# Chunkwise mLSTM stage: steps written out, M rows spread by DMA, head-by-head exponentials and key weights on ScalarE

## Time and profile before

| | us |
|---|---|
| median of 3 runs | 1765.7 |
| the profiled execution, its device time | 1764.76 |
| its span in the trace | 1763.1 |
| the mLSTM block in it, from the last operation of `mlstm_gates` (415.7) to the first of `mlstm_norm` (545.3) | 129.6 |

### The profile page before, as it was taken

How to read it: one execution, slowest core, us unless ns; L and a number is a source line. 1 busy time by engine, 2 the same in 40 slices (tenths; PEclk the granted TensorE clock), 3 DMA queues, 4 the chain that set the end, 5 groups by cost and what they waited for, 6 DMA issues and landing times. The chain is left out here.

```text
span 1763.1 us, 20516 instructions
## 1 busy us (share of the span) xinstructions
PE 1534.4 (87%) x7374; PEld 843.3 (48%) x7375; DVE 605.9 (34%) x1060; ACT 331.0 (19%) x566; POOL 111.9 (6%) x113
## 2 busy tenths in 40 slices
PE   5999999957885798999899931999999999999968
PEld 1455544425773485665555521444444444444423
DVE  1222135435888333333376761011111111111107
ACT  1111122212223233343321110111111111111111
POOL 0000000000002000000000004011111111111100
PEclk7899999987987799999999955999999999999989
DMA  9101011050005102000041108687888987999937
GB/s 367 69 24 36 0 13 36 24 191 1 0 0 196 51 0 96 0 0 0 15 150 60 71 26 355 260 356 277 346 319 331 403 336 315 417 415 366 422 142 295
DMA packets 81139, 298.89 MB, mean 170 GB/s; under 512 B 18092, under 2 KB 28360, under 8 KB 71891
## 3 DMA queue, kind: packets, MB, share of 16 engines
q1 hardware_dynamic: 72356, 280.70, 40.7%
q0 software_dynamic: 8608, 16.84, 2.7%
q10 hardware_dynamic: 146, 0.98, 0.2%
HBM read 283.50 MB, written 25.73 MB: 175 GB/s over the span
## 5 line engine op out<-in xcount | busy, mean ns | idle before, releaser
L399 PE MATMUL ps<-w_in_tok,uT_tiles 128*128 128x512 f32 (+2 forms) x512 | 191.5, 535 | 1.2 <-ACT uT_tiles L320 1.2
L1712 PE MATMUL ps<-w_gate_sb,x_slotsT 128*128 x320 | 144.3, 604 | 9.7 <-issue 9.7
L1728 PE MATMUL ps<-w_down_sb,hidT 128*128 x320 | 148.0, 605 | 0.0
L399 PEld LDWEIGHTS ps<-w_in_tok,uT_tiles 128*128 128x128 f32 x512 | 97.7, 192 | 89.8 <-issue 61.1
L1712 PE MATMUL ps<-w_up_sb,x_slotsT 128*128 x320 | 140.6, 592 | 0.0
L1904 DVE TENSOR_TENSOR hid<-silu_g,ps 128x512 f32<-128x512 f32 x20 | 13.8, 688 | 294.4 <-PE ps L1712 294.4
L1419 PE MATMUL ps<-w_out,hT 128*128 128x512 f32 x256 | 114.2, 600 | 0.0
L480 PE MATMUL ps<-uT,mod 128*128 128x512 f32 x256 | 110.1, 592 | 1.7 <-ACTq L487 1.7
L1712 PEld LDWEIGHTS ps<-w_gate_sb,x_slotsT 128*128 128x128 f32 x320 | 59.8, 192 | 86.9 <-issue 86.9
L1712 PEld LDWEIGHTS ps<-w_up_sb,x_slotsT 128*128 128x128 f32 x320 | 60.8, 190 | 76.5 <-issue 76.5
L1728 PEld LDWEIGHTS ps<-w_down_sb,hidT 128*128 128x128 f32 x320 | 57.5, 189 | 66.5 <-issue 65.6
(11 more groups left out here) (377 smaller groups left out, 1966.9 us busy)
## 6 DMA issues: line engine op xcount, KB each, us to landing
light_gate_sb<-in_w_gate SPq DMA_DIRECT2D x20, 2048.0 KB, 11.4
light_up_sb<-in_w_up SPq DMA_DIRECT2D x20, 2048.0 KB, 16.5
light_down_sb<-in_w_down SPq DMA_DIRECT2D x20, 2048.0 KB, 13.1
w_gate_sb<-in_w_gate SPq DMA_DIRECT2D x12, 2048.0 KB, 11.5
w_up_sb<-in_w_up SPq DMA_DIRECT2D x12, 2048.0 KB, 15.9
w_down_sb<-in_w_down SPq DMA_DIRECT2D x12, 2048.0 KB, 21.5
uT<-in_w_ada SPq DMA_DIRECT2D x8, 2048.0 KB, 9.8
y_pair<-expert_rows SPq DMA_DIRECT2D x8, 1024.0 KB, 10.5
```

The lines of the kernel that those rows point to most:

```text
L399: mm = nc.tensor.matmul(ps[:, 2 + g, 0:n], uTt[:, j, k, :], wt[:, k, c0:c0 + n], start=k == 0, stop=k == KD - 1)
L1712: m = m_.matmul(ps[:, bank, :], xT[:, k, :], wt[:, bass.ds(buf, 1), k, :].rearrange("p a f -> p (a f)"), start=k == 0, stop=k == KD - 1)
L1728: m = m_.matmul(ps[:, 5 + half, :], hT[:, k, :], wd[:, bass.ds(buf, 1), k, half * 512:half * 512 + 512].rearrange("p a f -> p (a f)"), sta ...
```

The new lists, cut to their core (`HALVES` are the 16 pairs (i, d) in order, d innermost):

```diff
+                sp.wait_ge(s_rdy, 2)
+                sp.dma_start(self.md.rearrange("d h t -> h d t"), Mrow[:]).then_inc(s_mst, 16)
+                sp.wait_ge(s_mst, 16)
...
+            def _(sp):
+                for i, d in HALVES:
+                    if i > 0:
+                        sp.wait_ge(S["mm"][d], i)
+                        sp.wait_ge(S["a"][d], i)
+                    sp.dma_start(mb[:, d], self.md[d][:, cols(i, d)].partition_broadcast(P)).then_inc(s_mb[d], 16)
...
+                def decays(i, d):
+                    c = chunk(i, d)
+                    act.wait_ge(S["mm"][d], i + 1)
+                    if i > 0:
+                        act.wait_ge(S["p"][d], i)
+                    for h in range(H):
+                        op = a.activation(w[:, d, h, :], mm_[:, d, h, :], ACT.Exp, bias=self.acol[:, d, c, h:h + 1], scale=-1.0)
+                    op.then_inc(S["w"][d], 1)
+                    act.wait_ge(s_mb[d], 16 * (i + 1))
+                    if i > 0:
+                        act.wait_ge(S["q"][d], i)
+                    for h in range(H):
+                        op = a.activation(ab[:, d, h, :], mb[:, d, h, :], ACT.Exp, bias=self.mext[:, d, c + 1, h:h + 1], scale=-1.0)
+                    op.then_inc(S["a"][d], 1)
+
+                def keys(i, d):
+                    if i == TT - 1:
+                        return
+                    act.wait_ge(S["kt"][d], i + 1)
+                    if i > 0:
+                        act.wait_ge(S["cm"][d], i)
+                    for h in range(H):
+                        op = a.mul(kw[:, d, h, :], ps[:, 2, h * P:(h + 1) * P], self.wg[:, d, chunk(i, d), h:h + 1])
+                    op.then_inc(S["kw"][d], 1)
+
+                decays(0, 0)
+                decays(0, 1)
+                keys(0, 0)
+                keys(0, 1)
+                decays(1, 0)
+                for k in range(len(HALVES)):
+                    if k + 2 < len(HALVES):
+                        keys(*HALVES[k + 2])
+                    if k + 3 < len(HALVES):
+                        decays(*HALVES[k + 3])
...
+                def inner(i, d):
+                    if i > 0:
+                        pe.wait_ge(S["p"][d], i)
...  (scores to bank d)
+                    if d == 1:
+                        pe.wait_ge(S["kw"][0], i + 1)
+                    elif i > 0:
+                        pe.wait_ge(S["kw"][1], i)
...  (turned keys to bank 2)
+                def outer(i, d):
+                    pe.wait_ge(S["p"][d], i + 1)
+                    pe.wait_ge(S["q"][d], i + 1)
...  (and for cn of this direction, h of the half before; then the output as L798 to L801)
+                    pe.wait_ge(S["kw"][d], i + 1)
...  (and for cn of the half before; then the state product as L805 to L807)
+                inner(0, 0)
+                inner(0, 1)
+                pe.wait_ge(s_c0, 1)
+                for k, (i, d) in enumerate(HALVES):
+                    outer(i, d)
+                    if k + 2 < len(HALVES):
+                        inner(*HALVES[k + 2])
...
+                def masked(i, d):
+                    dve.wait_ge(s_mb[d], 16 * (i + 1))
+                    if i > 0:
+                        dve.wait_ge(S["w"][d], i)
+                    v.tensor_tensor(mm_[:, d], mb[:, d], self.c((C_MFW, C_MBW)[d]).unsqueeze(1).to_broadcast([P, H, P]), ALU.add).then_inc(S["mm"][d], 1)
...  (weighted: p and qs as L836 and L841; rows: as L849 to L852)
+                    for h in range(H):
+                        op = v.scalar_tensor_tensor(out=cst8[:, d, h, :], in0=cst8[:, d, h, :], scalar=self.dec[:, d, chunk(i, d), h:h + 1],
+                                                    in1=ps[:, 5 + h // 2, (h % 2) * hn:(h % 2 + 1) * hn], op0=ALU.mult, op1=ALU.add)
+                    op.then_inc(S["cn"][d], 1)
...
+                masked(0, 0)
+                masked(0, 1)
+                weighted(0, 0)
+                weighted(0, 1)
+                masked(1, 0)
+                for k, (i, d) in enumerate(HALVES):
+                    if k + 3 < len(HALVES):
+                        masked(*HALVES[k + 3])
+                    rows(i, d)
+                    state(i, d)
+                    if k + 2 < len(HALVES):
+                        weighted(*HALVES[k + 2])
```

More of the change, by code:

```diff
@@ L632, in _ @@
                     dve.wait_ge(s_m, d + 1)
[L633 removed]
+                    v.tensor_tensor(Mrow[:, d, :], mrow[:, d, :], rows[:, 2, :], ALU.subtract).then_inc(s_rdy, 1)
                     dve.wait_ge(s_rdy, d + 1)
@@ L736, in mlstm @@
         nc, ps = self.nc, self.ps
-        N = ("kc", "mb", "sc", "kt", "mask", "z", "w", "y", "a", "p", "q", "kw", "o", "cm", "cn", "h")
+        N = ("mm", "w", "a", "sc", "kt", "p", "kw", "q", "o", "cm", "h", "cn")
         S = {n: [self.sem(f"ml_{n}{d}") for d in range(2)] for n in N}
+        s_mb = [self.sem(f"ml_m_spread{d}") for d in range(2)]
         s_v, s_c0 = self.sem("ml_dve"), self.sem("ml_state0")
@@ L743, in mlstm @@
             sb = lambda n, s: self.sb(n, s, ctx=x)
-            kc, mm_, w, ab, p, q, kw = (sb(n, [P, 2, H, P]) for n in ("kc", "Mm", "W", "ab", "pT", "qs", "kw"))
+            mb, mm_, w, ab, p, q, kw = (sb(n, [P, 2, H, P]) for n in ("m_spread", "Mm", "W", "ab", "pT", "qs", "kw"))
             cst8 = sb("Caug", [P, 2, H, HD + 1])
@@ L747, in mlstm @@
             hn = HD + 1
-            chunk = lambda i, d: i if d == 0 else i * -1 + (TT - 1)
+            HALVES = [(i, d) for i in range(TT) for d in range(2)]
+            chunk = lambda i, d: i if d == 0 else TT - 1 - i
+            cols = lambda i, d: slice(chunk(i, d) * P, (chunk(i, d) + 1) * P)
+            @block.sync
+            def _(sp):
[4 more added lines that the diff above has]
+                    sp.dma_start(mb[:, d], self.md[d][:, cols(i, d)].partition_broadcast(P)).then_inc(s_mb[d], 16)
             @block.scalar
@@ L768, in _ @@
                 t = nc.tensor
-                for n in ("kt", "o", "cm"):
-                    for d in range(2):
-                        pe.sem_inc(S[n][d], 1)
-                pe.wait_ge(s_c0, 1)
[L773 to L808, removed]
@@ new lines, in inner @@
+                def inner(i, d):
+                    if i > 0:
+                        pe.wait_ge(S["p"][d], i)
+                    for h in range(H):
+                        m = t.matmul(ps[:, d, h * P:(h + 1) * P], self.qkT[:, 4 + h, cols(i, d)], self.qkT[:, h, cols(i, d)], start=True, stop=True)
+                    m.then_inc(S["sc"][d], 1)
+                    if i == TT - 1:
+                        return
+                    if d == 1:
+                        pe.wait_ge(S["kw"][0], i + 1)
+                    elif i > 0:
+                        pe.wait_ge(S["kw"][1], i)
+                    for h in range(H):
+                        m = t.transpose(ps[:, 2, h * P:(h + 1) * P], self.qkT[:, 4 + h, cols(i, d)], self.c(C_ID))
+                    m.then_inc(S["kt"][d], 1)
@@ new lines, in outer @@
+                def outer(i, d):
+                    c = chunk(i, d)
+                    pe.wait_ge(S["p"][d], i + 1)
+                    pe.wait_ge(S["q"][d], i + 1)
+                    if i > 0:
+                        pe.wait_ge(S["cn"][d], i)
+                    if d == 1:
+                        pe.wait_ge(S["h"][0], i + 1)
+                    elif i > 0:
+                        pe.wait_ge(S["h"][1], i)
+                    for h in range(H):
+                        o = ps[:, 3 + h // 2, (h % 2) * hn:(h % 2 + 1) * hn]
+                        t.matmul(o, p[:, d, h, :], self.vaug[:, c, h, :], start=True, stop=False)
+                        m = t.matmul(o, q[:, d, h, :], cst8[:, d, h, :], start=False, stop=True)
+                    m.then_inc(S["o"][d], 1)
+                    if i == TT - 1:
+                        return
+                    pe.wait_ge(S["kw"][d], i + 1)
+                    if d == 1:
+                        pe.wait_ge(S["cn"][0], i + 1)
+                    elif i > 0:
+                        pe.wait_ge(S["cn"][1], i)
+                    for h in range(H):
+                        m = t.matmul(ps[:, 5 + h // 2, (h % 2) * hn:(h % 2 + 1) * hn], kw[:, d, h, :], self.vaug[:, c, h, :], start=True, stop=True)
+                    m.then_inc(S["cm"][d], 1)
@@ new lines, in weighted @@
+                def weighted(i, d):
+                    dve.wait_ge(S["sc"][d], i + 1)
+                    dve.wait_ge(S["w"][d], i + 1)
+                    if i > 0:
+                        dve.wait_ge(S["o"][d], i)
+                    v.scalar_tensor_tensor(out=p[:, d], in0=ps[:, d, :].rearrange("p (h t) -> p h t", h=H), scalar=QSCALE, in1=w[:, d],
+                                           op0=ALU.mult, op1=ALU.mult).then_inc(S["p"][d], 1)
+                    dve.wait_ge(S["a"][d], i + 1)
+                    v.scalar_tensor_tensor(out=q[:, d], in0=self.qkT[:, 0:H, cols(i, d)], scalar=QSCALE, in1=ab[:, d],
```

(21 more changed lines are left out.)

52 lines of the change are left out of this document (5 added, 47 removed).

## The result

The changed kernel takes 1725.9 us, the median of four executions (1722.4 to 1728.4), beside 1763.6 for the kernel before on the same chip: a ratio of 0.978, 95% interval 0.9761 to 0.9799. The forecast was 1728.

A forecast was written before the change was run, and what follows sets the result against it. Bound: VectorE's passes and TensorE's products in a ring through shared banks, no engine full. Second output at 434.5, + 3.2 + 64.0 + 4.7 + 3.6 - 1.5, ends at 508.5 instead of 545.0: 1728 us, range 1714 to 1742 (1750 with rivals).

The forecast's parts named there:

- a ring of three halves: mLSTM scan: rows, TensorE products, keys, exponentials, M load and mask close a loop of 10.40 + L; 4.57 us a half.
- a half of 5 to 6 us: Sign of being wrong in size: a hand-over or fetching the written-out lists costs more, with clock and landing as forecast.
- ring without the load, for three halves: mLSTM scan: rows, hand-overs, TensorE products, keys, exponentials and mask, everything but the M load, claimed at 10.40 us.
- landing L: Time for the DMA spread of M rows, 256 KB in 512 pieces, to land: 3.3 us, bounds 2.7 and 4.1.
- one half more at the lower level: TensorE still at its lower clock for one half after the second output could start: + 3.2 us.
- a share of 0.18 later: Share of the scan's later time with TensorE at the lower clock, from today's mean of 0.91: + 4.7 us.
- VectorE idle 0.3 to 1 us before each mask: Expected sign in the changed profile: VectorE waits for the spread M rows, 0.3 to 1 us a half.
- The keys: Key weights put on ScalarE at 1.0 us; on VectorE, 0.61, its sum would be 5.01 and the time some 6 us later.
- Written-out lists: Scan loops written out as instruction lists: nothing charged for fetching them; a cost named as a possible miss.
- the first one: Clock rival: TensorE at its lower clock throughout gives 1765, chance 0.09; half of the time low 1739, chance 0.10.
- The second, a slow spread: Rival: 128 partitions reading the same 2 KB land late; L about 8 gives 1750, chance 0.05; from 13 up, 0.06.
- The store of the rows: M rows stored before the scan: costs nothing, with 13.9 us of cover; without cover at most 12.7.

## Why the prediction came out

The time was right, within 2 us, and so was the main claim: a ring of three halves, not an engine, sets the pace. Four runs that act on it alone (two M tiles, contiguous rows, exponentials first, loaded twice) move the block by -14 to +29 us as it says. Inside the sum, errors of opposite sign met, so that the agreement within 2 us is in part luck. The prediction gave a half of 5 to 6 us, with clock and landing as forecast, as the sign of a dearer hand-over or of the fetching of the lists; 5.17 came, but with a landing outside its bounds.

| step | forecast | measured |
|---|---|---|
| block | 92.8 | 91.2 |
| second output, after the block's start | 18.8 | 18.5 |
| ring without the load, for three halves | 10.40 | 9.86 |
| landing L | 3.3 (2.7 to 4.1) | 4.5 median, 5.64 in the round shown |
| VectorE alone, a half | 4.40 | 4.01 at most |
| TensorE alone, a half | 4.28 | 4.01 at most |
| keys and exponentials | 3.52 with a hand-over | 3.46 |
| second to fourteenth output, a half | 4.57, with the low clock 5.2 | 5.17 |
| last output to the end | 3.6 | 3.63 |

**The term that was mis-sized is L.** It lies outside the bounds that I gave. I had placed it between loads of other sizes and piece counts; the run with contiguous rows shows that pieces count, 1.4 us for 384 more of them. Why the 512 pieces land later than the 3.9 us of `mod`, with pieces of the same size and twice the bytes, no run settles.

**What made up for it is the clock.** I charged 3.2 us for one half more at the lower level after the second output, and 4.7 for a share of 0.18 later. The second output already ran at the full clock (0.39 for two products, 0.64 for those of the first), and only two of the four rounds have a low stretch: 4.24 us from output to turned keys became 5.83 (458.21 to 464.04), so 1.6 each, 3.2 in all in place of 7.9. Over the twelve halves from the second output: 4.57 x 12 = 54.9; the load + 6.1, as those that the masks waited for took 4.5, 5.6, 4.7 and 4.5 in place of 3.3; the rest of the ring - 2.2 (four times 0.54); the clock + 3.2. Together 62.0, and 62.0 were measured (432.46 to 494.44).

**Shape.** I forecast VectorE idle 0.3 to 1 us before each mask. In fact it waits 2.0 to 3.0 us before every third one and hardly between: outputs come as little as 4.01 us apart, the engines' pace (463.87 to 467.88), and then one comes after 6 to 7. The average hid pauses of over 2 us on TensorE, and both falls of its clock in this stretch come after such a pause.

**The keys.** Here the step failed. I let VectorE's sum decide, and priced the keys on VectorE at 6 us more; the run gave 5.6 less by the ratios and 6.9 less in the block. The sum of VectorE does grow by 0.62, but the pace was the ring's, and I had counted the keys as part of it without asking what the ring is worth without them. With two M tiles the keys on ScalarE give 4.01 a half against 4.63, so what decides is whether a ring passes through the pass. The Trainium skill, "ScalarE: Activation LUTs", section "Rules for kernel authors", sends multiplications to VectorE: that gave the shorter block in this kernel, though the reason that the runs show is the ring.

**Written-out lists** were charged at nothing, and a cost was feared; alone they save 5.9 us of the block. Part of it shows in VectorE's sum: in the changed kernel, too, it takes 1.21 us from denominator to state (456.77 to 457.98), not the 1.34 taken from the earlier trace rows.

**The rivals.** The clock stayed at 0.95 in the steady part, so the first one is out. The second, a slow spread, was the right thing to fear: the load is the wait that came, at 4.5 and not at 11.

The store of the rows is hidden, as forecast: issued at 397.4, landed 2.1 us later, and the block begins at 413.9.

## What to carry to other kernels

A load into a tile with one buffer closes a ring through everything that must happen before the tile is free, and that ring, divided by the halves it spans, can be the pace while every engine has slack: add it up from the trace, and look first for a second buffer or an order that takes steps out of it. Price a spread by its pieces as well as its bytes, and store what is read again in the order in which it is read. Before moving a pass to an engine with more slack, ask which ring it joins there.

## What the runs showed of the hardware

The same 256 KB spread over 128 partitions landed 4.5 us after its issue in 512 pieces of 512 bytes, and 3.1 in 128 pieces of 2 KB (medians of sixteen loads); two in a row, 1024 pieces, took 8.2 from the second one's issue.

TensorE's granted clock didn't follow the length of its pauses alone. In the changed kernel it fell to 0.50 with pauses of 2.65 and 2.35 us and not with 1.91 and 2.09; with the spread loaded twice it fell with 3.41, 3.67, 3.59 and 3.92 and not with 3.03 and 2.71; with all passes back on VectorE there were nine pauses of 2.01 us before an output, and it fell after two of them. With pauses of 1.6 us and less it stayed at 1.00 from the second output on (two M tiles, contiguous rows, keys on VectorE).
